# Six layer norms taken bank by bank: the last two down units are interleaved, the normalizing step moves forward, and the stream is transposed in halves into the upper PSUM banks

## The reference

```
for l in range(2):
    x = layer_norm(ALPHA * x + 0.5 * swiglu(x, ffn_w1[l, 0], ffn_w2[l, 0]), ln_g[l, 0], ln_b[l, 0])
    mix = hybrid_mixer(x, w_in[l], ...)
    x = layer_norm(ALPHA * x + mix, ln_g[l, 1], ln_b[l, 1])
    x = layer_norm(ALPHA * x + 0.5 * swiglu(x, ffn_w1[l, 1], ffn_w2[l, 1]), ln_g[l, 2], ln_b[l, 2])
```

## Time and profile before

| | |
|---|---|
| median of 3 executions | 2121.34 us (2117.25 to 2124.5) |
| the profiled execution | 2121.39 us, of which 2119.4 us are the span of instructions |
| PE matmul busy | 1874.8 us (88%) |
| DVE busy | 1388.9 us (66%) |
| ACT busy | 950.3 us (45%) |
| mean granted clock of PE | 0.928 of full speed |

### The profile page before, as it was taken

One profiled execution on the slowest core, in us unless ns is written; L12 is line 12 of the kernel. 1 busy time (PEld: TensorE's weight loads), 2 busy tenths in 40 slices (PEclk: granted clock), 3 DMA queues, 4 the chain that ended last, 5 costly groups with the idle time before them and its releaser, 6 DMA issues.

```text
span 2119.4 us, 31329 instructions
## 1 busy us (share of the span) xinstructions
PE 1874.8 (88%) x12399; PEld 1721.0 (81%) x12399; DVE 1388.9 (66%) x1399; ACT 950.3 (45%) x858; POOL 145.5 (7%) x156
## 2 busy tenths in 40 slices
PE   7998999989998999899998999799773788878885
PEld 7998999979997999799997999599463667667764
DVE  6445677676666454686857666758737667667765
ACT  4443656434333434466533434334223555555553
POOL 1000000000000000000000000100003211112111
PEclk9999999999998999899999999799676999989998
DMA  6554454637674555455554766333121867777773
GB/s 242 187 190 158 161 197 164 241 132 263 250 261 157 179 178 180 157 179 197 216 182 162 274 239 234 112 130 131 39 68 63 305 258 265 279 270 286 294 276 136
DMA packets 61909, 418.16 MB, mean 197 GB/s; under 512 B 7312, under 2 KB 7680, under 8 KB 13952
## 3 DMA queue, kind: packets, MB, share of 16 engines
q1 hardware_dynamic: 51392, 369.19, 47.9%
q0 software_dynamic: 10416, 47.79, 6.5%
q10 hardware_dynamic: 16, 0.01, 0.0%
HBM read 405.94 MB, written 11.02 MB: 197 GB/s over the span
## 4 chain that ended last, share of the span: by engine, by line
PE 81%; DVE 5%; issue 4%; POOL 3%; POOLq 2%; DVEq 2%; ACT 2%; DMA 1%; ACTq 0%
PE ps L1496 15%; PE ps L1498 15%; PE ps L1497 15%; PE ps L1523 5%; PE ps L1524 5%; PE ps L1527 5%; PE ps L756 3%; PE ps L757 3%; PE ps L758 3%; PE ps L740 2%; POOLq L555 1%; POOL tests L553 1%; PE ps L785 1%; PE ps L787 1%; PE ps L786 1%
## 5 line engine op out<-in xcount | busy, mean ns | idle before, releaser
L1781 DVE TENSOR_TENSOR wlo<-raw,whi 128x2048 fp32r<-128x2048 f32 x236 | 538.1, 2290 | 355.8 <-ACT whi L1630 353.0
L1496 PE MATMUL ps<-xThi,whi 128*128 128x256 f32 x2400 | 686.0, 286 | 11.2 <-DVE xTlo L1792 8.3
L1497 PE MATMUL ps<-xTlo,whi 128*128 128x256 f32 x2400 | 684.2, 285 | 0.0
L1498 PE MATMUL ps<-xThi,wlo 128*128 128x256 f32 x2400 | 684.0, 285 | 0.0
L1630 ACT ACTIVATE whi<-raw 128x2048 fp32r<-128x2048 f32 x236 | 449.9, 1910 | 380.6 <-PE ps L1498 271.5
L1496 PEld LDWEIGHTS ps<-xThi,whi 128*128 128x128 f32 x2400 | 466.0, 194 | 15.5 <-issue 11.7
L1497 PEld LDWEIGHTS ps<-xTlo,whi 128*128 128x128 f32 x2400 | 466.0, 194 | 1.8 <-issue 0.2
L1498 PEld LDWEIGHTS ps<-xThi,wlo 128*128 128x128 f32 x2400 | 465.7, 194 | 0.0
L1247 DVE TENSOR_TENSOR wlo<-raw,whi 128x2048 fp32r<-128x2048 f32 x75 | 172.7, 2309 | 24.7 <-ACT whi L917 24.4
L917 ACT ACTIVATE whi<-raw 128x2048 fp32r<-128x2048 f32 x76 | 145.6, 1917 | 48.1 <-PE ps L758 25.6
L1524 PE MATMUL ps<-wlo,hhi 128*128 128x512 f32 x352 | 137.5, 391 | 0.0
(11 more groups left out here) (418 smaller groups left out, 2792.8 us busy)
## 6 DMA issues: line engine op xcount, KB each, us to landing
raw<-stream SPq DMA_DIRECT2D x236, 1024.0 KB, 4.9
raw<-experts SPq DMA_DIRECT2D x76, 1024.0 KB, 6.8
mod<-experts SPq DMA_DIRECT2D x38, 1024.0 KB, 6.2
adaraw<-ada POOLq DMA_DIRECT2D x24, 1024.0 KB, 5.1
yd<-lnrow POOLq DMA_DIRECT2D x19, 512.0 KB, 6.8
lnrow<-ln_g POOLq DMA_DIRECT2D x6, 512.0 KB, 5.3
lnrow<-ln_b POOLq DMA_DIRECT2D x6, 512.0 KB, 6.4
x_sb<-x SPq DMA_DIRECT2D x1, 1024.0 KB, 5.1
```

The lines of the kernel that those rows point to most:

```text
L1496: nc.tensor.matmul(outs[tile], wh, xh[:, k, :], start=k == 0, stop=False)
L1497: nc.tensor.matmul(outs[tile], wh, xl[:, k, :], start=False, stop=False)
L1498: last = nc.tensor.matmul(outs[tile], wl, xh[:, k, :], start=False, stop=k == KD - 1)
L1781: v.tensor_tensor(wlo[:, slot, :], raw[:, slot, :], whi[:, slot, :].bitcast(F32), ALU.subtract).then_inc(lo_done, 1)
```

## The change

Five things change, all at the six norms.

1. The last two down units are interleaved bank by bank (`last_rows`). Each bank of a unit is a part of six matmuls. The order is: unit A bank 4, A bank 5, B bank 4, B bank 5, A bank 6, B bank 6, A bank 7, B bank 7. `y0_done` is counted after the B part of banks 4, 5 and 6; unit A counts as used after its bank 7, unit B at the end.
2. `norm` on DVE takes 512 columns at a time (`summed`), and computes the moments of the first token tile and its subtraction and gain (`centred(0)`) before the second tile's sums.
3. The scaled stream is written in four pieces of 512 columns, in the order of `PIECES`: both tiles' lower columns, then both tiles' upper columns. The two lower `xTlo` pieces are made before the fourth stream piece.
4. The transposes write banks 4 to 7 (`transpose_stream`, `stream_banks`). The first unit behind a norm starts in a feed-forward with the lower half of the features (`first_unit`), in the mixer with the products of `xThi` (`first_half_unit`).
5. The PE loop over the steps of a feed-forward is cut differently: its body is now down, gate and up, four times, with the first and the last step outside. The order of the units stays. In the second block one group of banks is renamed.

The core of the diff; the edits that are left out rename banks in the setup and call the new functions on ACT.

```
@@ -226,6 +226,12 @@
         def halves(b, n=1):
 
             return banks(b, n).rearrange("p (c t) -> p c t", t=T)
+        def stream_banks(i):
+            return banks(4 + 2 * i, 2).rearrange("p (k t) -> p k t", t=P)
+        PIECES = [(0, 0), (1, 0), (0, 1), (1, 1)]
 
...
+            def first_unit(rnd, slot, outs, n):
+                for half in range(2):
+                    pe.wait_ge(xTlo_done, n * 4 + (2 * half + 2))
+                    if half == 0:
+                        weights_ready(rnd, slot)
+                    for tile in range(2):
+                        for k in range(4 * half, 4 * half + 4):
+                            c = k * 256 + tile * P
+                            wh, wl = whi[:, slot, c:c + P], wlo[:, slot, c:c + P]
+                            nc.tensor.matmul(outs[tile], wh, xThi[:, k, :], start=k == 0, stop=False)
+                            nc.tensor.matmul(outs[tile], wh, xTlo[:, k, :], start=False, stop=False)
+                            last = nc.tensor.matmul(outs[tile], wl, xThi[:, k, :], start=False, stop=k == KD - 1)
+                last.then_inc(used, 1)
+            def first_half_unit(rnd, slot, outs, n):
+                for tile in range(2):
+                    for k in range(KD):
+                        if tile == 0 and k % 4 == 0:
+                            pe.wait_ge(xThi_done, n * 4 + (2 + k // 2))
+                        if (tile, k) == (0, 0):
+                            weights_ready(rnd, slot)
+                        c = k * 256 + tile * P
+                        nc.tensor.matmul(outs[tile], whi[:, slot, c:c + P], xThi[:, k, :], start=k == 0, stop=False)
+                        nc.tensor.matmul(outs[tile], wlo[:, slot, c:c + P], xThi[:, k, :], start=False, stop=False)
+                    for k in range(KD):
+                        if tile == 0 and k % 4 == 0:
+                            pe.wait_ge(xTlo_done, n * 4 + (2 + k // 2))
+                        c = k * 256 + tile * P
+                        last = nc.tensor.matmul(outs[tile], whi[:, slot, c:c + P], xTlo[:, k, :], start=False, stop=k == KD - 1)
+                last.then_inc(used, 1)
...
+            def last_rows(units, parts, before):
+                def part(j, bank_no):
+                    (rnd, slot), (hh, hl) = units[j], parts[j]
+                    i, n = bank_no // 2, bank_no % 2
+                    if bank_no == 0:
+                        weights_ready(rnd, slot)
+                        pe.wait_ge(*before[j])
+                    for k in range(2):
+                        h, lo = hh[:, k, i * P:(i + 1) * P], hl[:, k, i * P:(i + 1) * P]
+                        c = k * D + n * 512
+                        nc.tensor.matmul(bank(4 + bank_no), h, whi[:, slot, c:c + 512], start=False, stop=False)
+                        nc.tensor.matmul(bank(4 + bank_no), h, wlo[:, slot, c:c + 512], start=False, stop=False)
+                        ins = nc.tensor.matmul(bank(4 + bank_no), lo, whi[:, slot, c:c + 512], start=False,
+                                               stop=j == 1 and k == 1)
+                    return ins
+                part(0, 0)
+                part(0, 1)
+                part(1, 0).then_inc(y0_done, 1)
+                part(1, 1).then_inc(y0_done, 1)
+                part(0, 2)
+                part(1, 2).then_inc(y0_done, 1)
+                part(0, 3).then_inc(used, 1)
+                part(1, 3).then_inc(used, 1)
+            def transpose_stream(n):
+                for j, (i, b) in enumerate(PIECES):
+                    pe.wait_ge(x_done, n * 4 + (j + 1))
+                    for k in range(4 * b, 4 * b + 4):
+                        last = nc.tensor.transpose(stream_banks(i)[:, k, :], x[:, i, k * P:(k + 1) * P], eye[:, :])
+                    last.then_inc(xT_ps, 1)
...
             def ffn(base, f, n):
-                pe.wait_ge(xTlo_done, n * 4 + 4)
-                cols_unit(*at(base, 0), xThi, xTlo, [bank(0, 0, T), bank(1, 0, T)])
+                first_unit(*at(base, 0), [bank(0, 0, T), bank(1, 0, T)], n)
                 cols_unit(*at(base, 1), xThi, xTlo, [bank(0, T), bank(1, T)])
                 pe.wait_ge(setup_dve, 2)
                 open_sums()
-                with pe.Fori(0, FFN_STEPS // 2) as i:
+                def gate_up(rnd, o, par):
+                    cols_unit(*at(rnd, o), xThi, xTlo, [bank(2 * par, 0, T), bank(2 * par + 1, 0, T)])
+                    cols_unit(*at(rnd, o + 1), xThi, xTlo, [bank(2 * par, T), bank(2 * par + 1, T)])
+                def down_proj(rnd, o, par, count):
+                    pe.wait_ge(hlo_done, count)
+                    rows_unit(*at(rnd, o), hhi[:, par], hlo[:, par], False, False)
+                gate_up(base, 2, 1)
+                with pe.Fori(0, FFN_STEPS // 2 - 1) as i:
                     for s in range(2):
-                        o, par = 2 + 3 * s, 1 - s
-                        cols_unit(*at(base + 2 * i, o), xThi, xTlo, [bank(2 * par, 0, T), bank(2 * par + 1, 0, T)])
-                        cols_unit(*at(base + 2 * i, o + 1), xThi, xTlo, [bank(2 * par, T), bank(2 * par + 1, T)])
-                        pe.wait_ge(hlo_done, f * FFN_STEPS + 2 * i + s + 1)
-                        rows_unit(*at(base + 2 * i, o + 2), hhi[:, 1 - par], hlo[:, 1 - par], False, False)
-                pe.wait_ge(hlo_done, (f + 1) * FFN_STEPS)
-                rows_unit(*at(base, UNITS_FFN - 1), hhi[:, 0], hlo[:, 0], False, True)
+                        down_proj(base + 2 * i, 4 + 3 * s, s, f * FFN_STEPS + 2 * i + s + 1)
+                        gate_up(base + 2 * i, 5 + 3 * s, s)
+                down_proj(base, UNITS_FFN - 5, 0, (f + 1) * FFN_STEPS - 2)
+                gate_up(base, UNITS_FFN - 4, 0)
+                last_rows([at(base, UNITS_FFN - 2), at(base, UNITS_FFN - 1)], [(hhi[:, 1], hlo[:, 1]), (hhi[:, 0], hlo[:, 0])],
+                          [(hlo_done, (f + 1) * FFN_STEPS - 1), (hlo_done, (f + 1) * FFN_STEPS)])
 
             pe.wait_ge(eye_in, 16)
-            transpose_x(0, x)
...
 @@ -1582,7 +1665,10 @@
-                            cols_unit(rnd, slot, xThi, xTlo, [bank(b, 0, T), bank(b, T)])
+                            if u == 0:
+                                first_half_unit(rnd, slot, [bank(b, 0, T), bank(b, T)], l * 3 + 1)
+                            else:
+                                cols_unit(rnd, slot, xThi, xTlo, [bank(b, 0, T), bank(b, T)])
@@ -1609,12 +1695,15 @@
                         cols_unit(*at(base, i), ybhi, yblo, [bank(q, 0, T), bank(q, T)])
-                    else:
+                    elif q < 2:
                         pe.wait_ge(mlo_done, l * 4 + q + 1)
-                        rows_unit(*at(base, i), xThi[:, 2 * q:2 * q + 2], xTlo[:, 2 * q:2 * q + 2], q == 0, q == 3)
-                transpose_x(l * 3 + 2, x)
+                        rows_unit(*at(base, i), xThi[:, 2 * q:2 * q + 2], xTlo[:, 2 * q:2 * q + 2], q == 0, False)
+                last_rows([at(base, UNITS_MERGE - 2), at(base, UNITS_MERGE - 1)],
+                          [(xThi[:, 2 * q:2 * q + 2], xTlo[:, 2 * q:2 * q + 2]) for q in (2, 3)],
+                          [(mlo_done, l * 4 + 3), (mlo_done, l * 4 + 4)])
+                transpose_stream(l * 3 + 2)
                 ffn(lay + OFF_FFN2 // RING, l * 2 + 1, l * 3 + 2)
-                transpose_x(l * 3 + 3, x)
+                transpose_stream(l * 3 + 3)
             pe_block2(pe, cols_unit, tokens_unit, rows_unit, transpose_x, open_sums)
 
 
...
+            def stream_lo(n, j):
+                i, b = PIECES[j]
+                dve.wait_ge(xThi_done, n * 4 + (j + 1))
+                ks, sl = slice(4 * b, 4 * b + 4), slice(i * P, (i + 1) * P)
+                v.tensor_tensor(xTlo[:, ks, sl], stream_banks(i)[:, ks, :], xThi[:, ks, sl].bitcast(F32),
+                                ALU.subtract).then_inc(xTlo_done, 1)
...
@@ -1808,32 +1911,52 @@
 
             def norm(n, units):
 
-                for i in range(TT):
-                    if i == 0:
-                        dve.wait_ge(y0_done, n + 1)
+                def summed(i, h):
+                    cs = slice(512 * h, 512 * h + 512)
+                    if (i, h) == (1, 1):
+                        dve.wait_ge(used, units)
                     else:
-                        dve.wait_ge(used, units)
-                    v.scalar_tensor_tensor(x[:, i, :], x[:, i, :], ALPHA, banks(4 + 2 * i, 2), ALU.mult, ALU.add)
+                        dve.wait_ge(y0_done, n * 3 + (2 * i + h + 1))
+                    v.scalar_tensor_tensor(x[:, i, cs], x[:, i, cs], ALPHA, bank(4 + 2 * i + h), ALU.mult, ALU.add)
                     dve.drain()
-                    for n2 in range(2):
-                        v.bn_stats(stats[:, i, n2, :], x[:, i, n2 * 512:(n2 + 1) * 512])
+                    v.bn_stats(stats[:, i, h, :], x[:, i, cs])
+                def moments(i):
                     dve.drain()
-                    ins = v.bn_aggr(mv[:, i, :], stats[:, i, :, :].rearrange("p a b -> p (a b)"))
```

(39 more changed lines are left out.)

39 lines of the change are left out of this document (21 added, 18 removed).

## The result

The changed kernel took 2106.74 us in the median of four runs (2105.04 to 2108.39), against 2120.49 us (2117.25 to 2124.5) before on the same chip: a ratio of 0.9934, with a 95% interval from 0.9914 to 0.9955. In a second comparison with more runs it was 0.9951 (0.9930 to 0.9972). The profiled execution took 2108.21 us (span 2106.3).

What follows compares the result with a forecast made beforehand. PE was taken to bound the first block, pausing only at six norms. Gains of 2.8 us (N1, N4) and 4.2 (N2, N5) less 4.3 lost (N3, N6) gave -2.7 us: 2118.7 us, range 2111.5 to 2124.

Steps and rivals of the forecast that it cites:

- S: First matmul of the next unit behind a norm; forecast at R + 5.8, against R + 7.03 at the first norm before.
- N1 and N4: First and fourth norms: forecast 1.4 us faster each, 0.2 from earlier moments and 1.2 from R to S.
- DVE's list: DVE's work at a norm from its start to the end of the moments: forecast about 7.6 us.
- R: Start of the first scaling at a norm, behind the moments and the root; at the first norm 211.93 before.
- N2 and N5: Second and fifth norms: PE's end governs; forecast 2.1 us faster each, 1.1 from moments and 1.0 up to S.
- E: End of the last down matmul ahead of a norm; only the gap from E to S was taken to change time.
- N3 and N6: Third and sixth norms: forecast losses of 2.1 and 2.2 us; 1.4 from later moments, then 0.7 and 0.8.
- signs of being wrong: Missing stall at N3 and N6, S before R + 5.5, or clock behind norms 1.00 or far longer at 0.50.
- Rival 1: Clock comes up with the transposes behind every norm: up to 9.4 us more gained; chance of half or more 0.2.
- Rival 2: Stall at N3 and N6 lets the clock fall during unit B: +0.9 us each, 2120.5 us; chance 0.15.
- rival 4: DVE's list is the bound at every norm, so nothing comes of the change: 2121 to 2123 us; chance 0.1.
- Rival 3: Inner loop's back edge is exposed at twelve jumps in the feed-forwards: +34 us, 2153 us; chance 0.04.

Runs made afterwards that it cites:

- the tables are early: Either kernel with POOL making one-hot tables ahead of an even block's row store, not the odd one's: kernel before 2026.14 us (0.9555), changed kernel 2023.82 us (0.9542).

## Why the prediction was wrong

**What failed first: the second block.** The prediction took it as unchanged, since the code of its stages is but for the entry, and so its sum held only norms. The cut of TensorE's loop, which I had listed with the edits at the norms though it stands at none, and had entered at nothing but for a rival, alone gave 7 us. This is shown (the cut alone, 0.9966), and that PE's wait for the tables falls with it from 79.5 to 70.8 us in the experts' loop. Its way is shown halfway. Shorter drains and shorter waits of PE go together, and the gain is gone once the tables are early. That sooner loads make the drains shorter is argued from the packets, not tried. Why another form of TensorE's loop in the first block goes with sooner loads in the second is not shown. Moving TensorE's code by 127 waits, growing POOL's program or TensorE's, and another arrival time did not bring the difference about; where data and code lie in memory was not tried.

**The sum for the norms.** With the drains off the path the change gives 2.3 us, and I had said 2.7. That is luck, since two errors cancel there. Each norm is counted from the first start of its last two down units to S:
- N1 and N4 gave 1.9 us each (23.85 to 21.93) and not 1.4. Moments at 208.95 were right (209.17, less the 0.3 by which the scales differ), DVE's list of 7.6 us too (7.55). S came at R + 5.35 and not R + 5.8: I had let the first unit wait for the end of the last transposes, and it starts 0.5 to 0.8 us behind their start.
- N2 and N5 gave 2.3 each (forecast 2.1): moments at E + 1.77 for E + 1.75, with the idle stretch of under 1 us ahead of the last half (0.73). S at R + 5.62.
- N3 and N6 lost 2.0 and 1.85 (forecast 2.1 and 2.2). E came 1.9 us later, as forecast, though my own numbers (656.96 less 655.18) give 1.8. The branch cost what was forecast, 0.8 us more behind the moments.
- Together that is 4.7 us of gain for 2.7. Missing altogether was the attention stage, which gave 2.5 us back while the clock was low there for longer.

Two of my signs of being wrong came true: S before R + 5.5 at N1 and N4, and a granted clock of 1.00 behind them.

**PE's waits.** I had said that the wait for the stream at the first transposes would fall from 42.5 to near 35 us, and it is 34.4. What I had not entered is that the piece that DVE makes behind two `xTlo` costs a new wait of 1.22 us at each norm, so that the whole line of the view stays at 41.7.

**The clock.** Rival 1 came true at N1 and N4 in some executions and not in others, while N5, which had kept its clock, had 3.4 low us behind S. So it was right to leave it out of the sum as chance, and wrong to treat a kernel's six stretches as its own: two executions of the kernel before differ at N2 by 3.4 us at the low clock. Rival 2 did not come: from the stall at N3 to E the clock is 1.00, and behind S 5.5 us were cold where 5.4 had been. Nor did rival 4: DVE waited for PE at N2. Rival 3, the exposed back edges, did not come either: in the cut loop they cost nothing. The layer loop's branch did cost, 3.5 us, and writing the loop out gives them back. By the Trainium skill (Runtime: NRT & Kernel Launch, Instruction fetch mechanics) a taken branch waits for a fetch when its target lies out of the fetched window; the trace agrees for that one branch only, with 16 KB of instructions loaded inside its 3.78 us.

**The bound for no change.** Single times of the kernel before reach 0.4% to either side of their median, so 0.3% was about right for medians of three. Most of that scatter seems to be that of the drains: 2113 to 2130 us with them on the path (30 executions), 2025.4 to 2028.1 with them off it (five).

## What to carry to other kernels

Unchanged code is not unchanged time: where a stage waits on transfers that meet by chance, first take that wait off the path, and then measure the change; here one line for it was worth 95 us, the whole change 2.3. Split a transfer of data between engines only together with a consumer that starts on the parts, since finer pieces without it were 5 us slower here. Where a profile shows "issue" behind a jump, try to write the loop out; here it was worth 5.9 us, of which 3.3 are the jump and the rest goes with the clock.

## What the runs showed of the hardware

- A drain on POOL behind a store ended with the store's last packets: in all 48 such drains of six profiles it ends 0.4 to 0.6 us behind the start of the last one. DVE's work around the store starts at the same distance from it to 0.05 us, but for one instruction that came 0.35 us later in three of the six, and still the drains run from 5.6 to 10.8 us. In the 10.6 us one, all but nine of 144 packets had started by 5.9 us; the rest came from 6.8 us on, in steps of 0.46 or 0.16 us, until 10.2. A store's packet takes 0.16 us and one of a load 0.31, together 0.47, so the late share seems to have taken turns with loads. By the Trainium skill (DMA: Bandwidth & Descriptors, Issuing engines are not separate DMA queues) transfers of all issuers interleave on the same engines; the steps of 0.46 us agree.
- The Trainium skill (SBUF — State Buffer, Who interferes with whom) lets two-input work of DVE block GpSimd's reads. The 1.63 us of the `oneh` addition after, against 0.72 in the quieter case, fit that (DVE wrote a `wlo` from two tiles until 1729.5), but the scatter of the drains does not come from it, with DVE the same in all.
- A wait on a raised semaphore cost TensorE 54 ns late in its program; with 127 of them at the start the first matmul came at 9.6 us, where it comes at 6.6 to 7.7 in the other profiles.
